# The down product of a convolutional FFN as seven block products over pairs of token tiles, in three weight groups, with the results added and stored by GpSimd

## The reference

```python
def conv_ffn(h, conv_state, w_up, w_conv, b_conv, w_down):
    u = h @ w_up                                   # 1024 -> 2 * 2816
    ...
    a, g = jnp.split(uc, 2, axis=-1)
    out = (jax.nn.silu(a) * g) @ w_down            # 2816 -> 1024: the down product
    return out, padded[:, -(CONV_W - 1):]
...
    f_out, conv_new = conv_ffn(h2, conv_state, p['w_up'], p['w_conv'], p['b_conv'], p['w_down'])
    x = x + g2 * f_out
```

## Time and profile before

| | |
|---|---|
| Median of 3 runs | 3029.07 us (3028.74 to 3031.07) |
| Span of the profiled execution | 3031.5 us |
| TensorE busy | 2948.6 us (97%) |
| VectorE busy | 1759.8 us (58%) |
| ScalarE busy | 1207.0 us (40%) |
| GpSimd busy | 586.9 us (19%) |
| Mean granted clock of TensorE | 0.987 of full speed |
| Down product on TensorE, start of the first matmul to the end of the last | 2504.5 to 3020.5 us |

### The profile page before, as it was taken

One profiled execution on the slowest core, in us unless ns is written; L12 is line 12 of the kernel. 1 busy time (PEld: TensorE's weight loads), 2 busy tenths in 40 slices (PEclk: granted clock), 3 DMA queues, 4 the chain that ended last, 5 costly groups with the idle time before them and its releaser, 6 DMA issues.

```text
span 3031.5 us, 48232 instructions
## 1 busy us (share of the span) xinstructions
PE 2948.6 (97%) x17353; PEld 2562.3 (85%) x17353; DVE 1759.8 (58%) x2649; ACT 1207.0 (40%) x2325; POOL 586.9 (19%) x609
## 2 busy tenths in 40 slices
PE   7999999999999999899998999999999999999998
PEld 5878888887777888888888999999999998887886
DVE  2300016733998999795667777777877775234222
ACT  4611112223776888454554333333423233113110
POOL 3310003312666777220110000000000000002000
PEclk8999999999999999999999999999999999999999
DMA  6322224544522251796654444444666676335331
GB/s 217 112 79 73 72 70 157 159 133 112 132 58 58 59 103 36 233 322 204 197 181 171 154 152 153 153 150 157 189 208 217 207 235 233 130 116 186 130 127 55
DMA packets 321026, 446.38 MB, mean 147 GB/s; under 512 B 68994, under 2 KB 220360, under 8 KB 314086
## 3 DMA queue, kind: packets, MB, share of 16 engines
q1 hardware_dynamic: 304616, 394.94, 41.1%
q0 software_dynamic: 14928, 49.38, 4.8%
q10 hardware_dynamic: 1332, 0.06, 0.0%
HBM read 289.20 MB, written 155.10 MB: 147 GB/s over the span
## 4 chain that ended last, share of the span: by engine, by line
PE 51%; DVE 4%; DMA 2%; issue 1%; ACT 1%; SPq 0%; DVEq 0%; ACTq 0%; POOL 0%
PE facc L2600 26%; PE dacc L2709 15%; PE eacc L2579 6%; DMA w_out_plain<-w_out 1%; PE mpT L2726 1%; PE mpm L2735 1%; PE eyT L2562 0%; PE mpS L2745 0%; PE exT L2592 0%; DVE drows L2306 0%; PE mpT L2776 0%; DVE fV L2238 0%; DMA fraw<-w_up 0%; DMA dring<-w_down 0%; PE mpN L2761 0%
## 5 line engine op out<-in xcount | busy, mean ns | idle before, releaser
L2709 PE MATMUL dacc<-drows,dact 128*128 128x512 f32 (+1 forms) x2200 | 511.1, 394 | 4.7 <-DVE dact L2312 1.2
L2709 PEld LDWEIGHTS dacc<-drows,dact 128*128 128x128 f32 (+1 forms) x2200 | 407.8, 186 | 107.6 <-POOL drows L1783 3.2
L767 PE MATMUL pacc<-pring,h1H 128*128 128x512 f32 x1360 | 431.9, 394 | 3.4 <-ACT h1H L326 3.4
L2600 PE MATMUL facc<-fright,fsums 128*128 128x416 f32 x2112 | 417.8, 353 | 9.6 <-ACT facc L1846 6.6
L2600 PEld LDWEIGHTS facc<-fright,fsums 128*128 128x128 f32 x2112 | 398.0, 189 | 15.4 <-issue 7.3
L1123 DVE TENSOR_TENSOR_SCAN aC<-aB,aC,a 128x512 f32<-128x512 f32 (+3 forms) x326 | 362.8, 1113 | 12.1 <-ACT aB L1079 1.1
L1183 POOL TENSOR_TENSOR aS<-aS,aC 128x512 f32<-128x512 f32 (+3 forms) x326 | 335.1, 1036 | 151.9 <-DVE aC L1123 145.5
L767 PEld LDWEIGHTS pacc<-pring,h1H 128*128 128x128 f32 x1360 | 256.8, 189 | 56.2 <-ACT h1H L326 3.5
L2600 PE MATMUL facc<-fright,fwH 128*128 128x416 f32 x1056 | 290.2, 356 | 8.8 <-DVE fU L2222 6.9
L1750 POOL DMA_DIRECT2D y_out<-dy x34 | 18.5, 543 | 1383.3 <-DVE dy L2329 1383.3
L767 PE MATMUL pacc<-pring,h1L 128*128 128x512 f32 x640 | 248.0, 389 | 0.0
(11 more groups left out here) (329 smaller groups left out, 4976.7 us busy)
## 6 DMA issues: line engine op xcount, KB each, us to landing
sums_d<-fsums SPq DMA_DIRECT2D x88, 512.0 KB, 2.9
fsums<-sums_d SPq DMA_DIRECT2D x88, 512.0 KB, 4.7
dact_plain<-act_d SPq DMA_DIRECT2D x32, 1408.0 KB, 6.4
fraw<-w_up SPq DMA_DIRECT2D x66, 512.0 KB, 4.1
proj_out<-pstage SPq DMA_DIRECT2D x119, 256.0 KB, 2.0
qk_T<-pturn POOLq DMA_DIRECT2D x68, 256.0 KB, 3.1
mwa<-w_ada SPq DMA_DIRECT2D x16, 1024.0 KB, 6.8
aq<-qk_T SPq DMA_DIRECT2D x28, 512.0 KB, 11.9
```

The source lines that it names most:

```text
L767: op = mm_(acc[:, n % NB], h[:, kk, tok(t)], weight(q, w), start=(j == 0), stop=(j == len(order) - 1))
L2600: mm = nc.tensor.matmul(bank, a[:, kk], b[:, kk], start=(begins and kk == 0 and m == 0), stop=(kk == count - 1 and m == 2), skip_group_che ...
L2709: mm = nc.tensor.matmul(down_acc[0:rows, n % 2], at[:, l, kk, 0:rows], r, start=(kk == 0 and m == 0), stop=(kk == NF - 1 and m == len(pass ...
```

## The change

The down product gets the same form as the up product. Tile t and tile t + 8 make a pair (`HALF` = 8 pairs), the output's two column halves are the other axis, and the 22 channel rows fall into three groups of 2 times 3, 2 times 4 and 2 times 4 rows (`GROUPS`). A unit is one pair in one group: 24 units, seven products each, with 9 or 12 matmuls (512 columns) to a product. Unit w takes the residual, which from the second group on is the sum that the group before has stored in `x1_d`, adds its gated results and stores it back, in the last group to y.

```diff
+    GROUPS = ((0, 3), (6, 4), (14, 4))
+    HALF = NPT // 2
+    UNITS = len(GROUPS) * HALF
+    PRODUCTS = ("P1", "P5", "P6", "P2", "P7", "P3", "P4")
+    LEFTS = ("A11", "S1", "A12", "S3", "S2", "S4", "A22")
...
+            def load_act(w):
+                g, p, k0, s = unit(w)
+                if w == 2:
+                    sp.wait_ge(left_low, 7)
+                elif w > 2:
+                    sp.wait_ge(left_low, 7 * w)
+                to = part_first if w == 1 else part
+                for e in range(2):
+                    sp.dma_start(to[:, e, 0:2 * s], d["act_d"][p + HALF * e, :, k0:k0 + 2 * s, :]).then_inc(part_in, 16)
...
+            def load_res(w, j):
+                at_least(sp, res_stored[j], 16 * w)
...
+            for w in range(UNITS):
...
+                if w + 1 < UNITS:
+                    load_res(w + 1, 0)
+                if w + 1 < UNITS:
+                    load_res(w + 1, 1)
+                if w + 2 < UNITS:
+                    load_act(w + 2)
...
-            def store_y(n):
-                w, b = act_of(n)[1], n % 2
-                pool.wait_ge(out_ready, n + 1)
-                pool.dma_start(d["y_out"][tok(n % NT), cols(n)], y2[:, b]).then_inc(y_stored[b], 16)
+            def add_residual(w, j):
...
+                    pool.wait_ge(down_gated, 4 * w + j + 1)
+                    pool.wait_ge(res_in[j], 16 * w + 16)
+                    nc.gpsimd.tensor_tensor(res_of(w, j), res_of(w, j), y2_of(w, j), ALU.add).then_inc(out_ready, 1)
+                    pool.wait_ge(out_ready, 4 * w + j + 1)
...
+                pool.dma_start(d["y_out" if unit(w)[0] == 2 else "x1_d"][rows_, cols_], res_of(w, j)).then_inc(res_stored[j], 16)
...
+            def down_slot(w):
+                g, p = unit(w)[0:2]
+                change = p == HALF - 1 and g + 1 < len(GROUPS)
+                if change:
+                    next_sum(0, g + 1)
+                    next_sum(1, g + 1)
+                add_residual(w, 0)
+                if change:
+                    next_sum(2, g + 1)
+                add_residual(w, 1)
+                add_residual(w, 2)
+                if change:
+                    next_sum(3, g + 1)
+                add_residual(w, 3)
...
+            def finish_out(w, j):
...
+                dve.wait_ge(done[("P2", "P7", "P3", "P4")[j]], UP + w + 1)
+                at_least(dve, out_ready, 4 * w + j - 1)
+                if j in (0, 3):
+                    v.tensor_tensor(y_, down_a if j == 0 else down_b, gate_, ALU.mult).then_inc(down_gated, 1)
+                else:
+                    sem = c22_taken if j == 1 else c12_taken
+                    dve.wait_ge(e_taken, UP + w + 1)
+                    v.tensor_tensor(y_, down_b if j == 1 else down_c, five(w), ALU.add).then_inc(sem, 1)
+                    dve.wait_ge(sem, UP + w + 1)
+                    v.tensor_tensor(y_, y_, gate_, ALU.mult).then_inc(down_gated, 1)
...
+            def sample_down(g):
...
+                for n in range(2 * s):
+                    at = n if n < s else 4 + n - s
+                    for e in range(4):
+                        mm = nc.tensor.matmul(down_s[e * DEC:(e + 1) * DEC, 0:2 * P], sample_act[:, n],
+                                              raw_rows[:, at, 2 * P * e:2 * P * (e + 1)], start=(g == 0 and n == 0),
+                                              stop=(g == 2 and n == 2 * s - 1), skip_group_check=True)
...
+                    else:
+                        pe.wait_ge(c22_taken, UP + w + 1)
+                    three(banks[name], left(one, w)[0:2], cell(other, g)[0:2], name in ("P1", "P5"), done[name])
...
+                if w in (4, 6, HALF + 5):
+                    sample_down((4, 6, HALF + 5).index(w))
```

660 lines of the change are left out of this document (443 added, 217 removed).

## The result

The changed kernel takes 3074.34 us, the median of four runs (3072.70 to 3077.12), beside 3030.07 us for the kernel before on the same chip: a ratio of 1.0144, interval 1.013 to 1.0159. It is slower, by less than 2% but clear of the noise; 3011 us, faster, was forecast. The profiled execution's span is 3071.0 us, 39.5 us more than before.

The account below looks back on a forecast made before the run. TensorE was taken to bound the kernel: 438.3 us of work + 15 start + 5 loop + 36 passages + 5 clock = 499.3 for 516.0; with 1.4 gained at the end, 3011 us, range 2976 to 3036.

Parts of the forecast that it names:

- that rival: Sample products run one after the other, 51 us for 10.5, total 3051 us; 10%, shared with other waits that size.
- the hindrance itself: VectorE with two SBUF inputs and GpSimd reading SBUF take turns: start and passages 51 us, else some 18.
- The rival in which nearly all was hidden: Start and passages cost 6 + 8 + 4 us without hindrance, loop 3, clock none: 2971 us; 25%.
- The start: Units 0 and 1: late P6, P3 and P4 plus a second piece lose 15 us, bounds 6 and 20.
- Passages: Changes of weights at units 7 to 8 and 15 to 16: P6 waits for T2's low part, 20 + 16 us.
- T3's case: At the passages, GpSimd's T3 comes ahead as well: 45 us in all for both.
- They cost nothing unless they hold up an activation load behind them: SyncE's weight-row loads in units 3, 5 and 10, asked for at least a unit ahead: no cost in the sum.
- The loop in group one: Residual store, reload, activation load and sums take 15.2 us against 14.6 a unit: 5 us over some six units.
- this rival: The loop binds: slower store and load landings make it 42 us for 5, total 3048 us; 12%.
- Terms two and three: Apparently the weight-row loads, forecast to cost nothing, and the loop in group one, forecast at 5 us.
- The clock: Three long waits may lower TensorE's granted clock to the 1.2 GHz level: 5 us, from 0 to 10.
- The end: Last two outputs added on VectorE, two operations behind the last matmul for four: a gain of 1.4 us.

Follow-up runs that it names:

- the last run: Unread products in the passages' waits, added to the kernel with A22 in two buffers, all additions and sums on VectorE and T2 ahead of B21: 3042.85 us, 1.0035.

## Why the prediction was wrong

**What held.** The work of TensorE (441.3 for 438.3), the sample products side by side (10.8 for 10.5, so that rival is out), the hindrance itself, and that P6 of units 8 and 16 waits for VectorE's dT. The Trainium skill, "SBUF — State Buffer", section "Who interferes with whom", was right in both parts: the two engines exclude each other where both read, and a GpSimd instruction that only writes hinders nothing. The rows beside it are 4.97 us for a 0.69 us piece, and 2.28 us for a 2.28 us piece beside the constant. The rival in which nearly all was hidden is out with it.

**The start: 18.0 us for 15, in part by luck.** P6 of unit 0 started at 2514.98, where 2514 was forecast. But P3 did not wait for GpSimd's low part of B22 as forecast (4 us). P2 waited in its place, 4.06 us. It started 0.1 us behind VectorE's low part of B21, which it needs and whose three pieces took from 2514.74 to 2523.12 beside GpSimd's low parts of T3 and B22. P4 waited 2.53 us for 5, and 5.0 us went to the lower clock of three products, which the 15 us don't contain.

**Passages: mis-sized by 29 us (65.4 for 36).** The working took T1 as done before the activations land (8.4 us into unit 7) and T3 as coming later. They landed 4.8 us into it (2663.97), so VectorE met T1 (4.62) at once, and being slowed it met T3 too (4.51). GpSimd's prices were low as well: 4.5 to 4.95 for 4.2 at 2048 columns. 31.6 + 4.6 + 4.5 + some 1.5 is 42.2 us, near the 42.3 that lie between 2663.99 and P6's start at 2706.33. That it fits so well is luck: four of GpSimd's additions fell in there, not three, and not all of the work stood one after the other. P6 was late by 27 us for 20 in the first passage and by 23 for 16 in the second; T3's case was even named ("45 in all") and not taken.

That is half of the 29 us. The other half lies behind P6, where the working ended: P3 and P4 of the same unit wait for the low parts of B22 and T4 (1.6 and 2.2 us), and P6 and P4 run at the lower clock, 7 to 8 us a passage. That these two waits are for the low parts is read from the ends in the trace; no run took them away alone.

The hindrance is real, but it isn't the larger part. Without any computing of GpSimd 45 of the 65 us remain, with VectorE making the sums; with the sums replaced by a constant 34 do. The working gave 12 us for both passages without hindrance. So more than half of what the passages lose is VectorE's own work and the lower clock behind the waits for it.

**"They cost nothing unless they hold up an activation load behind them": they did.** The sum had no term for it. SyncE's loads of weight rows hold up the activation load and the residual reload that follow, P4 of units 4 and 6 waits 3.2 and 4.7 us, and the pieces of 1.5 to 2 MB take 10.7 us in the median to land. The store of the convolution's last rows, which stands on the same queue behind a reload that waits, was not looked at: 9.98 us of ScalarE in unit 2, and 6.64 of TensorE behind it. The run with P5's early place shows that such a wait is real, and it and the runs with the rows elsewhere show that much of it comes back at the next transfer in line.

**The loop in group one: right mechanism, low price, and a second loop left out.** The rival gave it 3.8 us a unit from landings of 11 us together on. In the chain of after the store's landing was 6.4 us and the load's 5.9 to 6.6, above that point, but only two of the five loads of group one were released that way. The others waited for A22's low part, a wait that `load_act` has and the working did not look at; landing and VectorE's work then make some 16 to 19 us from load to load. In the first half of group three the chain runs round that second loop alone (loads at 2924.66, 2945.55, 2965.96 and 2985.45), where it costs little: units of groups two and three that repeat take 19.5 to 20.3. Half of this rival, then, came true. Terms two and three together make the 20 us of units 2 to 6; they can't be told apart further, since taking one away lengthens the other.

**The clock: 5 us forecast, 21.9 by the lengths of 13 products.** The cause named was loads, but most waits of 2 to 15 us for VectorE or ScalarE did it too. Even the row that gave the price, 16 matmuls in 6.10 us, stood behind a wait for ScalarE. What of it is real cost stays open: filling the waits of the passages gave back 3.3 of 4.6 us, 3.1 of 6.3, and, in the last run, nothing of 4.7. It is already inside the other rows of the table.

**The end.** 1.4 us less was forecast; the time from the last product to the end of the span went from 11.0 to 12.0 us. The part that was worked out came true: the last store is issued 1.7 us behind the last product, where it was 3.2. From that issue to the end of the span it took 10.3 us for 7.8. What made that longer was not tried.

## What to carry to other kernels

Here fewer products helped only in the units that repeat. Price what happens where the weights change: add up the work of VectorE and GpSimd there as if they were one engine, from when the data *land*, with every GpSimd instruction that can fall in, and compare the sum with TensorE's time; here 42 us against 20. Go on to the last product that needs a new factor, not only to the first. Where both read SBUF, moving GpSimd's work to VectorE can win although VectorE is the fuller of the two. A load that is asked for early is not free: look at what stands behind it on its queue, and put the small transfer ahead of the large one. And where a load is released by several waits, price the loop of each.

## What the runs showed of the hardware

- The sample's activations (128 KB) landed 13.2 to 16.1 us after their issue behind 3 to 4 MB of weight rows on the queue, and 5.0 to 5.5 us when issued ahead of them. The rows of the changed kernel and of the run with earlier rows (there the first two of three):

```profile
DMA to landing us min/median/max: 13.2/14.2/16.1
```

```profile
DMA to landing us min/median/max: 5.0/5.3/5.5
```

- GpSimd's addition of 512 columns had a mean of 1659 ns over 86, where the earlier trace rows had 1188; the last two, with VectorE standing still beside them, took 1.28 and 1.29 us. TensorE's lower clock showed behind waits as short as 2.2 us: twelve matmuls took 4.57 us behind one, with a granted clock of 0.62, while twelve behind a wait of 2.27 us took 3.04.
- The 88 sample products of 256 columns, each on one of four blocks of 32 partitions, took 10.8 us, 0.12 us a product. The Trainium skill, "TensorEngine Tiling (Array Packing)", section "Key Properties", has a change of mode drain the array; with 10.8 us measured for 10.5 worked out and three entries and exits, no price of it can be seen.
